# The last pair of heads in a selected-key attention runs its four query tiles from the most keys to the fewest

## What is computed

```python
s_c = einsum('bghtd,bgnd->bghtn', qblk, kc) * scale + head_bias(t_pos - cmp_end)
p_c = masked_softmax(s_c, valid_c);  o_c = einsum('bghtn,bgnd->bghtd', p_c, vc)
...
s_s = einsum('bghtd,bgtld->bghtl', qblk, ks_g) * scale + bias_s
p_s = masked_softmax(s_s, dist_s >= 0);  o_s = einsum('bghtl,bgtld->bghtd', p_s, vs_g)
...
s_w = einsum('bghtd,bgkd->bghtk', qblk, kw) * scale + head_bias(dist_w)
p_w = masked_softmax(s_w, valid_w);  o_w = einsum('bghtk,bgkd->bghtd', p_w, vw)
return g0 * o_c + g1 * o_s + g2 * o_w
...
mix = concatenate([o_a, o_b], -1) @ w_out;  x = layer_norm(ALPHA * x + mix, ln1_g, ln1_b)
```

## Time and profile before

| | us |
|---|---|
| median of three runs | 3514.88 (3512.14 to 3516.32) |
| profiled execution | 3514.6 |
| its span | 3512.8 |
| TensorE busy | 3409.7 (97%) |
| VectorE busy | 1597.6 |
| ScalarE busy | 1259.8 |
| the changed stretch, first layer | about 2257 to 2377 |
| the changed stretch, second layer | about 2990 to 3104 |

### The profile page before, as it was taken

How to read it: one execution, slowest core, us unless ns; L and a number is a source line. 1 busy time by engine, 2 the same in 40 slices (tenths; PEclk the granted TensorE clock), 3 DMA queues, 4 the chain that set the end, 5 groups by cost and what they waited for, 6 DMA issues and landing times. The chain is left out here.

```text
span 3512.8 us, 47863 instructions
## 1 busy us (share of the span) xinstructions
PE 3409.7 (97%) x17592; PEld 2705.0 (77%) x17592; DVE 1597.6 (45%) x2814; ACT 1259.8 (36%) x2130; POOL 1362.2 (39%) x588
## 2 busy tenths in 40 slices
PE   8999999999999999999999999989999999899998
PEld 7888866788878888766788877757888787568886
DVE  5442445644235433353644255774331358743322
ACT  3222346522232223355322244463222353642222
POOL 3444222244434443322344433304444533134444
PEclk9999999999999999999999999999999999999999
DMA  4223321222323233211222332102222321112322
GB/s 157 96 94 98 113 67 37 72 96 96 95 87 101 96 96 112 92 61 37 90 96 94 98 121 74 67 19 77 96 96 94 120 83 50 49 54 96 96 96 90
DMA packets 86636, 303.58 MB, mean 86 GB/s; under 512 B 11189, under 2 KB 11701, under 8 KB 85342
## 3 DMA queue, kind: packets, MB, share of 16 engines
q1 hardware_dynamic: 86256, 301.56, 26.2%
q10 hardware_dynamic: 238, 0.09, 0.0%
HBM read 299.49 MB, written 4.74 MB: 87 GB/s over the span
## 5 line engine op out<-in xcount | busy, mean ns | idle before, releaser
L339 POOL TENSOR_TENSOR wL<-ring,wH 128x1024 fp32r<-128x1024 f32 (+1 forms) x509 | 1254.2, 2464 | 2082.8 <-ACT wH L329 1978.4
L289 PE MATMUL bank<-hH,wH 128*128 128x512 f32 x2448 | 965.7, 394 | 13.9 <-DVE yT L992 4.8
L329 ACT ACTIVATE wH<-ring 128x1024 fp32r<-128x1024 f32 (+1 forms) x518 | 543.7, 1050 | 1146.1 <-PE bank L291 961.5
L291 PE MATMUL bank<-hH,wL 128*128 128x512 f32 x2448 | 954.0, 390 | 0.0
L290 PE MATMUL bank<-hL,wH 128*128 128x512 f32 x2448 | 953.3, 389 | 0.0
L289 PEld LDWEIGHTS bank<-hH,wH 128*128 128x128 f32 x2448 | 460.0, 188 | 115.5 <-issue 6.3
L291 PEld LDWEIGHTS bank<-hH,wL 128*128 128x128 f32 x2448 | 459.8, 188 | 97.3
L290 PEld LDWEIGHTS bank<-hL,wH 128*128 128x128 f32 x2448 | 460.3, 188 | 94.7 <-issue 1.9
L289 PE MATMUL bank<-guH,wH 128*128 128x512 f32 (+1 forms) x1292 | 502.6, 389 | 2.1 <-ACT early L1388 1.4
L291 PE MATMUL bank<-guH,wL 128*128 128x512 f32 (+1 forms) x1292 | 496.1, 384 | 0.0
L290 PE MATMUL bank<-guL,wH 128*128 128x512 f32 (+1 forms) x1100 | 418.6, 381 | 0.0
(11 more groups left out here) (372 smaller groups left out, 3889.4 us busy)
## 6 DMA issues: line engine op xcount, KB each, us to landing
ring<-in_w SPq DMA_DIRECT2D x372, 512.0 KB, 3.6
ring<-in_down SPq DMA_DIRECT2D x96, 448.0 KB, 3.3
ring<-in_down SPq DMA_DIRECT2D x48, 512.0 KB, 3.6
ring<-in_next SPq DMA_DIRECT2D x15, 512.0 KB, 3.6
mix<-in_table SPq DMA_DIRECT2D x2, 2560.0 KB
mix<-spread SPq DMA_DIRECT2D x4, 768.0 KB, 7.2
ring<-in_first SPq DMA_DIRECT2D x5, 512.0 KB, 3.8
spread<-row SPq DMA_DIRECT2D x1, 2560.0 KB, 12.4
```

Of the source, the lines that this page charges most:

```text
L289: eng.matmul(out, a, hi, start=first, stop=False)
L291: return eng.matmul(out, b, hi, start=False, stop=last)
L329: eng.activation(parts_of(n, per)[0][:, 0:width], ring[:, n % NSLOT, 0:width], ACT.Copy).then_inc(w_hi, 1)
L339: eng.tensor_tensor(l[:, 0:width], ring[:, n % NSLOT, 0:width], h[:, 0:width], ALU.subtract).then_inc(w_lo, 1)
```

## The change

The tile of a step is taken from a new function. It gives the old tile for pairs 0 to 2, and 3, 2, 1, 0 for the last pair. Conditions that mean "first or second step of a pair" still go by u; those that mean "few keys" go by the tile. In ScalarE's `back` the wait for the PV pass now stands ahead of both forms of copy. Nothing is added or left out.

```diff
+        def pair_tile(u):
+            hp, i = divmod(u, NT)
+            return hp, NT - 1 - i if hp == NSA // 2 - 1 else i
+
         def scores(u):
-                hp, i = divmod(u, NT)
+                hp, i = pair_tile(u)
                 n = (i + 1) * P
-                if i == 0:
+                if u % NT == 0:
                     eng.wait_ge(tp_free, 13 + hp)
...
             def turn(u, w):
-                i = u % NT
+                i = pair_tile(u)[1]
...
-                        eng.wait_ge(p_back, 4 * (u - 1) + (2 * g + 2 if (u - 1) % NT < 2 else g + 3))
+                        eng.wait_ge(p_back, 4 * (u - 1) + (2 * g + 2 if pair_tile(u - 1)[1] < 2 else g + 3))
...
-                if u % NT < 2:
+                if pair_tile(u)[1] < 2:
                     turn(u, WIN)
                 if u and u % NT == 0:
                     pv(u // NT - 1)
...
-                if u % NT >= 2:
+                if pair_tile(u)[1] >= 2:
                     turn(u, WIN)
...
         def act_nsa(eng):
             def back(u):
-                hp, i = divmod(u, NT)
+                hp, i = pair_tile(u)
+                if u % NT == 0 and hp:
+                    eng.wait_ge(o_ready, hp)
                 if i < 2:
-                    if i == 0 and hp:
-                        eng.wait_ge(o_ready, hp)
```

More of the change, by code:

```diff
@@ L2456, in dve_nsa @@
                 if u < NU:
-                    hp, i = divmod(u, NT)
+                    hp, i = pair_tile(u)
                     n, r = (i + 1) * P, u % 3
                     c0 = S - P - i * P + CMP_END
-                    if u >= 5 and i == 1:
+                    if u >= 5 and u % NT == 1:
                         back_cmp(hp - 1)
@@ L2517, in act_nsa @@
                 if u < NU:
-                    i, r = u % NT, u % 3
+                    i, r = pair_tile(u)[1], u % 3
                     for o, (w, g) in enumerate(READ):
```

## The result

| | before | changed |
|---|---|---|
| median of 20 runs, us | 3514.89 (3509.83 to 3517.85) | 3519.38 (3514.09 to 3523.96) |
| span of the profiled execution, us | 3512.8 | 3520.3 |

The ratio is 1.0014 with a 95% interval of 1.0008 to 1.0020: 2.8 to 7 us slower, 4.5 by the medians, in the range and on the side forecast (+3.6). The interval does not reach 1, so the changed kernel is slower, by less than the 0.2% that the prediction called no change. The forecast was 3518.5 in a range of 3513 to 3524.

What follows compares the result with a forecast made beforehand. TensorE, busy 97% of the span, was taken as the bound. Seam +0.45, new wait +1.3, shorter scores -1.3 and the second wait with its copies gave +1.8 us per layer, +3.6 in both: 3518.5, range 3513 to 3524.

Steps and rivals of the forecast that it cites:

- The seam: Steps 10 to 12: four more transposes ahead of the PV pass of pair 2, so it ends later; +0.45 us per layer.
- the wait behind PV: After PV of pair 2, TensorE idles until ScalarE's copy frees the bank for step 12's window transposes; +1.3 us.
- the copies queued behind the exponentials of step 14: ScalarE's copies for step 13's window transposes wait behind 2.55 us of exponentials, from 83.65 to 86.2.
- the new end at bank 7: Last PV must wait until VectorE has taken the product tile from the same bank; starts 99.75 against 97.96.
- the second wait: TensorE idle before the window transposes of step 13, released by ScalarE's copy; 2.8 us.
- old hole: TensorE's 2.66 us wait for VectorE behind PV of pair 2, to be replaced by 2.8 before step 13's window transposes.
- Drop at the same place: Main case: clock falls at step 14's product tile as before; +1 to +3 us per layer, 3516.5 to 3521; chance 0.60.
- The full-clock variant: Tail behind PV of pair 2 without a clock drop: last PV at 98.2, +0.2 us per layer, 3515.3; chance 0.18.
- the shorter scores: Scores of step 15, run behind PV of pair 2, get shorter; -1.3 us per layer.
- The clock stays up: Rival: work cuts the time behind PV into pieces, no clock drop; +0.2 us per layer, 3515.3; chance 0.18.
- Down to the end: Rival: clock low from step 14's transposes on; +5.2 us per layer, 3525, up to 3537; chance 0.18.
- The waits simply go: Rival: tail waits and the clock's 1.6 leave, no wait enters; -5.7 us per layer, 3503.5; chance 0.04.

Runs made afterwards that it cites:

- Experiment 3: Changed kernel with ScalarE's weight copy of step 13 moved behind the copies of step 14; one execution, D 21.17 us in both layers.
- experiment 7: Changed kernel with the product tile of step 15 ahead of that step's transposes; one execution, D 20.0 and 19.78 us.
- experiment 4: Changed kernel with unread products filling idle TensorE before window transposes of steps 12 and 13: first fill (9, 20) 3517.62 us; second (5, 11) 3514.84 us, ratio 1.0003.
- experiment 1: Changed kernel with the product tiles of steps 14 and 15 moved to steps 13 and 14; 3512.57 us, ratio 1.0000 to the kernel before.
- experiment 8: Kernel before with product tiles in steps 13 and 14, and VectorE scaling probabilities of steps 14 and 15 first; 3507.8 us, ratio 0.9982.
- experiment 2: Kernel before, old tile order, with product tiles in steps 13 and 14 in place of 14 and 15; 3508.28 us, ratio 0.9990.

## Why the prediction was right, and where its sizes were off

Distances from the end of PV of pair 2, us:

| step | forecast | measured |
|---|---|---|
| end of PV of pair 2 later | +0.45 | +0.45 |
| TensorE idle until ScalarE's copy | 1.3 | 1.27 |
| exponentials of step 14 start | 3.82 | 3.86 |
| window transposes of step 13 start | 6.97 | 7.03 |
| VectorE takes the product tile of step 14 | 13.87 | 14.91 |
| to the compressed transpose | 1.3 | 1.25 |
| last PV starts, released by VectorE (D) | 19.9 | 20.9 |

- **Queues and places: right**, shown by the releasers in the trace and by moving single pieces. The seam, the wait behind PV, the copies queued behind the exponentials of step 14, and the new end at bank 7 came with their sizes. Experiment 3 moved the second wait's end by 0.94, the length of the copy that had stood ahead of it; experiment 7 took the last away, and ScalarE's copy became the end.
- **The clock: right that it falls, wrong from where, by 1.0 per layer.** I let it fall at the product tile, as before, and priced the stretch from the transposes of step 14 to the taking at 5.27 and a little. It fell some 3 us after PV's end already, so that the transposes of steps 13 and 14 ran slow too. Those fourteen took 3.35 where the forecast left them 2.34 (6.90 from their start to the taking, less the 4.56 that the slow tile had taken before); the tile itself took 4.53. By the granted clock of the stretches, TensorE was at 1.2 GHz for about 10.2 us in the changed kernel and 3.4 before, an estimate. The "old hole" was 1.88 and not 2.8 for the same reason: what stands in front of it was slower, the six transposes above all, which there cost nothing. This is the term of the sum that was too small: +1.8 forecast per layer, +2.77 measured. "Drop at the same place", as the main case has it, did not happen. The full-clock variant was priced at D 18.4 (pv at 98.2 for a PV end at 79.83); filled, it is 18.24.
- **The split of the sum.** The new wait at +1.3 and the shorter scores at -1.3 are no terms of their own: both lie ahead of the window transposes of step 13, which start at 7.03 behind PV's end whether TensorE is idle or filled there (experiment 4). ScalarE's queue sets that point. The total does not depend on this split, as it was walked and not added up.
- **The shares.** At full clock D is 18.24 changed and 16.98 before: +1.26 by waits. The clock costs 2.66 changed and 1.60 before: +1.06. The seam is +0.45. The sum is 2.77 by the way it is divided, so it proves nothing by itself; the shares rest on the fill's leaving the waits' ends where they were.
- **Rivals.** "The clock stays up" did not happen in the changed kernel. "Down to the end" did not happen in its profiled execution, where the clock was back within the product tile of step 14. But the last tile ran slow in experiment 3 and part of the last PV in experiment 1, so its chance was not idle. Of the other executions of the changed kernel only the mean clock is known, 0.990 to 0.992. "The waits simply go" fell; what it wanted is got by experiment 8, which gives VectorE's and TensorE's queues something else to do and leaves the tiles alone.

That both kernels are within 0.2% of each other was forecast and holds for the medians; the interval reaches just to it. That the medians differ by 4.5, nearer to the forecast's 3.6 than the 5.5 of the traces, is the scatter of executions and no merit of the forecast.

## What to carry to other kernels

Before reordering work of different sizes, look at what the slots of the schedule already hide: here the steps that had a filler (a product tile) between two dependent halves stood still while the large items moved to steps without one. Moving the filler (one line) gave 2.0 us per layer, moving the items cost 2.8. Follow each in-order queue past the moved piece, since a blocked copy delays everything behind it, and the engines that its pieces start in turn, and count which buffer the last producer shares with the consumer at the end.

## What the runs showed of the hardware

- A wait of 1.27 (1.28 in the first layer) right behind a PV pass, with eight transposes and scores behind it, was followed by a fall to 1.2 GHz in both layers of the changed kernel and of experiments 1, 3 and 7. A wait of 1.48 at another place was not, nor were 1.66 and 0.69 in experiment 2. The length of a single wait does not tell it.
- One full product of 128x128 by 128x128 in f32 took 0.23 at full clock in the first fill of experiment 4, as much as two transposes of the same size (0.12 each).
- VectorE's 128x6 TENSOR_TENSOR (L2431, L2436) takes 0.17 as a rule. In all eleven traces, once per layer, it started some 0.11 after GpSimd's 128x1024 TENSOR_TENSOR (2.35) and took 2.26 or 2.27, ending 0.02 or 0.03 after it; in experiment 3 it happened a second time in each layer, at 1.18. Beside the same GpSimd instruction, VectorE's 128x6 reciprocal (0.18) and its taking of a product tile from a bank (0.69) kept their length in experiment 3.
